# One layer with sampled latent attention: keys turned by VectorE in 32x32 blocks, scores in 32x32 tiles, inversion masks made by GpSimd

## The reference

```
# prompt, gated linear attention in chunks of 64 tokens
lower = where(strict, (kb @ kc^T) * decay, 0)
wy    = solve(eye + lower, eye)                 # unit triangular, 64x64
u, w  = wy @ vb, wy @ (kb * exp(gc))
for each of the 4 chunks: v_new = u - w @ S; o = ...; S = S * exp(g) + k^T v_new

# the 8 sequences, latent attention over 16 cached pages of 128 tokens
q_lat = einsum('bthd,rhd->bthr', q_nope, w_uk)
s     = (q_lat . lat + q_pe . kpe) * MLA_SCALE      # 4 heads, 256 + 64 wide
p     = softmax(s over the cached tokens and the new one)
o     = (p @ lat) @ w_uv

h = x + concat(y_gdn, y_mla) @ w_out
h = h + cross_attention(h, memory);  h = h + mixture_of_experts(h)
```

## Time and profile before

| | us |
|---|---|
| three timed runs | 1494.47, 1496.4, 1496.8 |
| median | 1496.4 |
| span of the profiled execution | 1494.2 |
| PE busy in the span | 1373.9 |
| DVE, ACT, POOL busy | 460.2, 201.1, 42.6 |
| inversion, scan, third stage | 153.6 to 202.0, 203.6 to 270.7, 270.7 to 320.3 |

### The profile page before, as it was taken

The page is one execution under the profiler, slowest core; times in us unless marked ns, Lnnn a source line. Parts: engine busy times, 40 slices in busy tenths (PEclk is TensorE's granted clock), DMA queues, the critical chain, the costliest instruction groups (busy, mean ns, idle before and its releaser), DMA issues.

```text
span 1494.2 us, 21159 instructions
## 1 busy us (share of the span) xinstructions
PE 1373.9 (92%) x8579; PEld 694.5 (46%) x8579; DVE 460.2 (31%) x1116; ACT 201.1 (13%) x399; POOL 42.6 (3%) x37
## 2 busy tenths in 40 slices
PE   8999899899998989999999988989989889899896
PEld 7668766555486453333333333333433333333332
DVE  1856643553024252113113112111221131122213
ACT  1053322321012440000000000000000000000002
POOL 0000101000000320000000000000000000000000
PEclk9999999999999989999999999999999999999999
DMA  9111534448365669999999999999999999999996
GB/s 367 39 53 57 199 143 149 184 150 329 141 253 180 225 276 413 389 413 424 426 425 424 428 425 424 427 424 426 425 424 429 423 424 426 424 426 427 424 426 245
DMA packets 96727, 490.73 MB, mean 328 GB/s; under 512 B 9307, under 2 KB 14527, under 8 KB 61626
## 3 DMA queue, kind: packets, MB, share of 16 engines
q1 hardware_dynamic: 94074, 468.89, 76.8%
q0 software_dynamic: 2304, 20.97, 3.6%
q10 hardware_dynamic: 296, 0.11, 0.0%
HBM read 484.01 MB, written 6.04 MB: 328 GB/s over the span
## 4 chain that ended last, share of the span: by engine, by line
PE 40%; DMA 18%; DVE 6%; issue 2%; SPq 1%; ACT 1%; POOL 1%; DVEq 0%
PE ps L2039 17%; DMA arena<-in_w_e 17%; PE ps L2076 14%; PE ps L2032 2%; PE ps L2064 1%; DVE arena L2604 1%; DVE arena L2614 1%; DVE arena L2611 1%; PE ps L2088 1%; DVE arena L2612 1%; SPq L1467 1%; DMA arena<-in_cache_mem_k 1%; PE ps L2104 1%; PE ps L2118 1%; PE ps L2112 0%
## 5 line engine op out<-in xcount | busy, mean ns | idle before, releaser
L2039 PE MATMUL ps<-arena 128*64 128x512 f32 x2048 | 454.3, 595 | 22.1 <-DMA arena<-in_w_e 21.5
L2039 PEld LDWEIGHTS ps<-arena 128*64 128x64 f32 x2048 | 148.9, 137 | 303.5 <-issue 278.5
L2076 PE MATMUL ps<-arena 128*64 128x512 f32 x952 | 214.2, 604 | 2.4 <-ACT arena L2291 2.4
L2076 PEld LDWEIGHTS ps<-arena 128*64 128x64 f32 x952 | 77.9, 141 | 136.1 <-issue 123.3
L2611 DVE TENSOR_SCALAR arena<-ps 128x1024 f32<-128x1024 f32 x15 | 18.4, 1225 | 243.5 <-PE ps L2039 243.5
L2032 PE MATMUL ps<-arena 96*128 96x512 bf16 x96 | 35.3, 488 | 46.0 <-DVE arena L2604 46.0
L2623 DVE COPY arena<-ps 128x512 f32<-128x512 f32 x15 | 10.4, 692 | 216.5 <-PE ps L2076 216.5
L2629 DVE TENSOR_TENSOR res<-res,ps 128x512 f32<-128x512 f32 x60 | 41.3, 688 | 115.9 <-PE ps L2088 115.9
L2025 PEld LDWEIGHTS ps<-arena 128*128 128x128 bf16 x768 | 49.5, 99 | 14.0 <-issue 12.2
L1753 PE MATMUL ps<-arena 128*128 128x512 f32 x128 | 55.8, 594 | 0.0
L2025 PE MATMUL ps<-arena 128*128 128x128 bf16 x768 | 54.0, 222 | 1.7 <-DVE arena L2578 1.7
(11 more groups left out here) (553 smaller groups left out, 1533.0 us busy)
## 6 DMA issues: line engine op xcount, KB each, us to landing
arena<-in_w_e SPq DMA_DIRECT2D x383, 1024.0 KB, 18.0
arena<-in_w_in SPq DMA_DIRECT2D x8, 1380.0 KB, 17.6
arena<-in_cache_mem_k SPq DMA_DIRECT2D x8, 1024.0 KB, 8.9
arena<-in_w_out SPq DMA_DIRECT2D x2, 2048.0 KB
arena<-in_w_xk SPq DMA_DIRECT2D x1, 4096.0 KB, 15.9
arena<-in_w_xv SPq DMA_DIRECT2D x1, 4096.0 KB, 13.8
arena<-in_w_xq SPq DMA_DIRECT2D x1, 4096.0 KB, 23.2
arena<-in_cache_mem_v SPq DMA_DIRECT2D x1, 4096.0 KB, 16.1
```

The source lines that it names most:

```text
L2039: last = pe.matmul(ps[64 * x:64 * x + 64, c, :], xe[:, k, 64 * x:64 * x + 64], weights[x][:, c * 512:(c + 1) * 512], start=False, stop=(k ...
L2076: last = pe.matmul(ps[64 * x:64 * x + 64, 4 + c, :], aT[:, k, 64 * x:64 * x + 64], weights[x][:, j * D + c * 512:j * D + (c + 1) * 512], s ...
```

## The change

The steps become 24, and what is in them changes. One, the queries of a sequence are scaled once and copied to four groups of 32 rows (`q_spread`, by a product with the constant `C_SAME`). Two, PE no longer turns keys: DVE transposes the gathered tiles in 32x32 blocks, one instruction of 128x1024 for a unit (a fifth of a sequence: 64 of its 320 feature columns, all 16 tiles), one step ahead, into one of four buffers. ACT copies nothing for it. Three, a unit's scores are eight products of K = 32, M = 4 and N = 512 (16 instructions), each on one 32x32 tile of the array; an even sequence uses tiles with equal row and column group, an odd one those two columns further, and 18 of the 24 steps hold a unit of each of two sequences, 4 hold one. A sequence has its own PSUM bank out of three. Four, the maximum is taken per partition by DVE, spread over the row groups by another `C_SAME` product, and reduced again; P is turned by DVE too. Five, the masks of the levels 1 to 5 are packed and made by POOL, behind the gathers of sequences 1 and 2. Six, there is a fourth slot for a sequence; sequence 3 is gathered when the last product of the inversion is done, the later ones after `pv_done` 1 to 4. Seven, the halves of `w_out` are loaded apart: the second at the start of the third stage, the first (the heads of the gated attention) when all values are done, because the fourth slot lies in its place.

```diff
-ARENA = 45680
+ARENA = 45680 + 3072 + 188
+SCRATCH = 4096
...
+    lat_slots.append(Arena(arena, AT_SLOTS + 6 * 1024).take([P, TILES, KVR]))
+    kr_slots.append(Arena(arena, AT_MORE).take([P, TILES, ROPE]))
...
-    def level_part(dve, m, t):
-        for half in HALVES:
-            mask = cst[half, C_LVL + m * P + half.start:C_LVL + m * P + half.stop]
-            last = nc.vector.tensor_tensor(CTc[half, t], LT[half, t, :, half], rep1(mask, [CHUNK, H, CHUNK]), ALU.mult)
-        return last
+    def level_part(eng, m, t):
+        return eng.tensor_tensor(CTc[:, t], LTc[:, t], rep1(c_(C_LVL + m * CHUNK, CHUNK), [P, H, CHUNK]), ALU.mult)
...
+                    pe.wait_ge(ml["q_apart"], 1)
+                    pe.matmul(ps[:, 3, 64:320], c_(C_SAME), q_apart[:, 0:256], start=True, stop=True)
+                    pe.matmul(ps[:, 3, 320:384], c_(C_SAME, P, ROPE), q_apart[0:ROPE, 256:320], start=True, stop=True).then_inc(ml["q_spread"], 1)
...
+    PIECES = 5
+    STEPS = PIECES * DEC // 2 + 4
+    def first_step(b):
+        return PIECES * (b // 2) + 2 * (b % 2)
...
+    def score_bank(b):
+        return 5 + b % 3
+    def pages_pe(pe, k):
+        here = step_units(k)
+        if here:
+            pe.wait_ge(sa["keys"], max(numbered[unit] for unit in here) + 1)
+            for b, m in here:
+                if m == 0 and b >= 3:
+                    pe.wait_ge(sa["exp"], b - 2)
+            for c in range(2):
+                for b, m in here:
+                    d = 2 * m + c
+                    for a in range(4):
+                        rows, out = slice(32 * a, 32 * a + 32), 32 * ((a + 2 * (b % 2)) % 4)
+                        last = pe.matmul(ps[out:out + H, score_bank(b), :], q_spread[rows, d, b, :],
+                                         KT[rows, numbered[b, m] % KEYS, c].rearrange("p s n -> p (s n)"),
+                                         start=(d == 0), stop=(d == 2 * PIECES - 1), tile_position=(32 * a, out))
             last.then_inc(sa["scored"], 1)
...
+            pe.wait_ge(sa["top"], b + 1)
+            if b > 0:
+                pe.wait_ge(sa["acc_moved"], b)
+            at = KVR + 4 * (b % 2)
+            pe.matmul(ps[:, 4, at:at + 4], c_(C_SAME), tops[:, b % 2], start=True, stop=True).then_inc(sa["spread"], 1)
+        for b in values_of(k):
+            pe.wait_ge(sa["p_turned"], b + 1)
...
+    def turn_keys_of(dve, k):
+        for b, m in step_units(k):
+            n = numbered[b, m]
+            if m == 0:
+                dve.wait_ge(seq_loaded[b % NSLOT], 32 * (b // NSLOT + 1))
+            if n >= KEYS:
+                dve.wait_ge(sa["scored"], units[n - KEYS][0] + 1)
+            rows = lat_slots[b % NSLOT][:, :, 64 * m:64 * m + 64] if m < 4 else kr_slots[b % NSLOT]
+            nc.vector.transpose(KT[:, n % KEYS], rows.rearrange("p s (c n) -> p c s n", c=2)).then_inc(sa["keys"], 1)
+    def pages_dve(dve, k):
+        for b in softmax_of(k):
+            dve.wait_ge(sa["scored"], k)
+            dve_chain.link(dve, nc.vector.tensor_reduce(lmax[:, b:b + 1], ps[:, score_bank(b), :], AX, ALU.max))
+            nc.vector.tensor_scalar(tops[:, b % 2], c_(C_GROUP, 4), lmax[:, b:b + 1], None, ALU.mult).then_inc(sa["top"], 1)
+        for b in values_of(k):
+            dve.wait_ge(sa["exp"], b + 1)
+            if b > 0:
+                dve.wait_ge(sa["pv_done"], b)
+            nc.vector.transpose(PT.rearrange("p s n -> p (s n)"), Pb).then_inc(sa["p_turned"], 1)
+        turn_keys_of(dve, k + 1)
+        for b in softmax_of(k):
+            at = KVR + 4 * (b % 2)
+            dve.wait_ge(sa["spread"], b + 1)
+            nc.vector.tensor_reduce(nmax[:, b:b + 1], ps[:, 4, at:at + 4], AX, ALU.max, negate=True).then_inc(sa["max"], 1)
...
-            for b in range(1, NSLOT):
+            for b in (1, 2):
                 load_sequence(pool, b)
-            for k in range(STEP_SCAN):
-                sampled_pool(pool, k)
+            for m in range(1, LEVELS):
+                for t in range(2):
+                    if m > 1:
+                        pool.wait_ge(y_made, 2 * (m - 2) + t + 1)
+                    level_part(nc.gpsimd, m, t).then_inc(c_ready, 1)
+            pool.wait_ge(uw_made, 3)
+            load_sequence(pool, 3)
...
-                    if m > 1:
-                        pe.wait_ge(c_ready, 2 * (m - 2) + t + 1)
+                    pe.wait_ge(c_ready, 2 * (m - 1) + t + 1)
...
-            for half in range(2):
-                load_w_out(sp, half)
+            load_w_out(sp, 1)
             store(sp, gdn_prompt[0, 0].rearrange("h k v -> k h v"), S[:, :, :])
-            sp.wait_ge(sa["pv_done"], DEC)
+            sp.wait_ge(sa["pv_done"], 6)
             sp.dma_start(memt, mem_prompt[0].rearrange("(t p) d -> p t d", p=P)).then_inc(mem_loaded, 16)
             sp.dma_start(wk, w_xk[0].rearrange("(k p) n -> p k n", p=P)).then_inc(wk_loaded, 16)
+            sp.wait_ge(sa["pv_done"], DEC)
+            load_w_out(sp, 0)
...
             pe.wait_ge(gn["placed"], 1)
+            pe.wait_ge(wout_loaded, 32)
             mix_part(0, range(H))
```

More of the change, by code:

```diff
@@ new lines, in build, with step_units @@
+    sa = {n: sem("smla_" + n, True) for n in ("keys", "scored", "top", "spread", "max", "exp", "p_turned", "pv_done", "acc_moved")}
+    PIECES = 5
+    STEPS = PIECES * DEC // 2 + 4
+    def first_step(b):
+        return PIECES * (b // 2) + 2 * (b % 2)
+    def step_units(k):
+        return [(b, k - first_step(b)) for b in range(DEC) if 0 <= k - first_step(b) < PIECES]
+    units = [(k, b, m) for k in range(STEPS) for b, m in step_units(k)]
+    numbered = {(b, m): n for n, (_, b, m) in enumerate(units)}
@@ new lines, in pages_act @@
+    def pages_act(act, k):
+        for b in softmax_of(k):
+            act.wait_ge(sa["max"], b + 1)
+            if b > 0:
+                act.wait_ge(sa["p_turned"], b)
+            for rows, dst in (((slice(0, P), slice(0, P)),), ((slice(64, P), slice(0, 64)), (slice(0, 64), slice(64, P))))[b % 2]:
+                last = nc.scalar.activation(Pb[dst, :], ps[rows, score_bank(b), :], ACT.Exp, bias=nmax[rows, b:b + 1],
+                                            accum_out=lsum[dst, b:b + 1])
+            last.then_inc(sa["exp"], 1)
+        for b in values_of(k):
+            act.wait_ge(sa["pv_done"], b + 1)
+            nc.scalar.copy(acc[:, b, :], ps[:, 4, 0:KVR]).then_inc(sa["acc_moved"], 1)
@@ L1155, in build, with level_step, head_step @@
+    def level_step(m):
+        return m - 1
+    STEP_SCAN = LEVELS
+    PER_CHUNK = 3
+    def chunk_steps(i, second):
+        k = STEP_SCAN + PER_CHUNK * i
+        return range(k + 1, k + PER_CHUNK) if second else range(k, k + 1)
+    STEP_HEAD = STEP_SCAN + PER_CHUNK * (SEQ // CHUNK)
+    def head_step(h):
+        return STEP_HEAD + 2 + h
+    assert head_step(H) == STEPS
     x_turned, x_ready = sem("inv_turned"), sem("inv_x_ready")
@@ L1244, in _ @@
                     last.then_inc(z_made, 1)
[L1245 to L1246 removed]
+            pages_pe(pe, level_step(LEVELS))
             for t in range(2):
@@ L1385, in join_exps @@
         act.wait_ge(jn["max"], 1)
-        nc.scalar.activation(part, part, ACT.Exp, scale=MLA_SCALE)
-        nc.scalar.activation(own, own, ACT.Exp, scale=MLA_SCALE).then_inc(jn["exp"], 1)
+        nc.scalar.activation(part, part, ACT.Exp)
+        nc.scalar.activation(own, own, ACT.Exp).then_inc(jn["exp"], 1)
     def join_weights(dve):
@@ L1549, in _ @@
         def _(pool):
-            for k in range(STEP_HEAD, STEPS):
-                sampled_pool(pool, k)
             pool.wait_ge(cx["q_made"], KD)
```

274 lines of the change are left out of this document (88 added, 186 removed).

## The result

Slower: 1518.28 us median of four runs (1514.24 to 1522.66) against 1495.67 for the kernel before (1494.47 to 1496.8, four runs). The ratio is 1.0152, 95% interval 1.0128 to 1.0176: 22.6 us too many, where 5.9 fewer were forecast, and outside the range.

A forecast was written before the change was run, and what follows sets the result against it. TensorE was taken to bound the three attention stages and DMA of expert weights the end, passing changes on one to one. Terms 0.5 - 5.0 - 4.9 - 5.5 + 6 + 3 = -5.9 gave 1490.5 us by the median, range 1481 to 1513.

The forecast's parts named there:

- before 153 us: Work ahead of the inversion: DVE gains five small operations and three products, loses half-masks; +0.5 us (0 to 1.5).
- inversion, to the end of PE: Inversion stage: first product waits for POOL's mask, then shorter levels; TensorE ends at 197.0 against 201.97, -5.0 us.
- barrier and scan, to the third stage: Scan: DVE sets about 15.0 us a chunk against 16.75, chunk 0 has a new wait; 62.1 against 67.0, -4.9 us.
- third stage, to 311.83: Third stage: six steps with turns and a last score, 15.2 us, become 8.1; -5.5 us (-7 to -2.5).
- to the memory keys: `w_out` and clock: After the last values: new wait for the first half of `w_out`, +6 us; lower clock after three new waits, +3.
- the wait for sequence 3: Scan, chunk 0: the gather lands at 206.8, TensorE waits 3 us and the next turn is late by 1.6.
- The clock: After three new waits (first level, chunk 0, `w_out`) TensorE runs at the lower clock: +3 us (0 to +5).
- the price of a double step: Attention scores: a step with two units, eight tiles side by side, 32 instructions, takes 2.0 us.
- four at once: Rival, score steps: two tiles in one row group take turns, a double step takes 3.8 us; 1513, chance 0.09.
- row tiles in turn: Rival, score steps: a sequence's four tiles write one bank in turn, 155 us in place of 43.6; some 1602, chance 0.04.
- two passes: Rival, DVE turns: a 32-bit transpose needs two passes, 2.45 us a turn; 1512, chance 0.10.
- the waits eat it: Rival: ISA instruction at 4.3, chunk 0 at 7, third stage at -2.5 add 7.8 us; 1498, chance 0.15.

The follow-up runs named there:

- the pad alone: A pad of 32 bytes a partition ahead of the arena, against the kernel before, nothing else changed: 1512.44 us, ratio 1.0115.

## Why the prediction was wrong, step by step

The sum is set against the starts of the stages in the two timelines (the earlier trace rows and above) and of the first memory key, before and after:

```profile
L1753 PE MATMUL ps<-arena x128: 592/592/697, 354.1 to 411.4; 128*128 128x512 f32 x128
```

```profile
L1739 PE MATMUL ps<-arena x128: 592/592/697, 355.7 to 413.0; 128*128 128x512 f32 x128
```

| term | forecast | measured |
|---|---|---|
| before 153 us | +0.5 | +2.4 |
| inversion, to the end of PE | -5.0 | -7.8 |
| barrier and scan, to the third stage | -4.9 | +3.9 |
| third stage, to 311.83 | -5.5 | -6.9 |
| to the memory keys: `w_out` and clock | +9 | +10 |
| experts and the end | 0 | +16.6 |

**The step that failed** is the one ahead of all terms: "what the three stages gain or lose, the end gains or loses one to one, and nothing is won in the last 930 us". It took the pace of the weight stream as given, since no line of that stage changes. But the change re-plans the memory of a partition, and the stream depends on where its destination begins: 425 GB/s on a multiple of 256 bytes, 417 to 418 at 32, 64 or 128 past it. That is 1.1% of the time, shown by the pad alone, and it is three quarters of the result. With the place repaired, one to one holds to about 1 us in the kernels above. The other quarter is the front, where a gain was forecast and 5.8 us were lost; the terms further down are about that.

The Trainium skill ("DMA: Bandwidth & Descriptors", How a descriptor splits into AXI transactions) says that a descriptor which does not start on a 256-byte boundary pays for the bytes from the boundary below it, and speaks there of reads. The unit of 256 agrees with the runs here, in which the source stays and the destination moves; whether the cause is that splitting no run here shows.

**The barrier was mis-sized.** The working kept the 1.64 us of before and put the wait for sequence 3 inside the scan, 3 + 1.6. As the program was written the landing was waited for at the block's end by every engine: 10.50, and the next score step at the lower clock (3.34 in place of 1.92). The scan itself, from 207.10 to 269.21, took 62.1 us against 67.1: the forecast's size, but by luck. The wait for sequence 3 and its 1.6 aren't in it; two costs that the working had not stand there instead, steps at the lower clock (3.41 for 1.92 at 234.27) and 3.01 us at the next barrier. And DVE didn't set the chunk at 15.0: one without such a step takes 13.2 us from one state subtraction to the next, near the 13.4 worked out for TensorE, and DVE waits for PE at both ends.

```profile
240.60 0.68 DVE L1272 TENSOR_TENSOR arena<-arena,ps 64x512 f32<-64x512 f32 x1 [2.53 <-PE ps L1295]
...
253.77 0.69 DVE L1272 TENSOR_TENSOR arena<-arena,ps 64x512 f32<-64x512 f32 x1 [0.79 <-PE ps L1295]
```

With the gather moved, the wait was where the working had it, but of 6.37 (5.89, 6.52 and 4.24 in the three kernels built on that one), for 3, at least in part since the gather, now behind the barrier, was issued 2.3 us after the inversion's end (200.55 against 198.28), where the working had it at that end.

**Before 153 us:** DVE was priced, PE not. The spreading of the queries, L695 and L696 at 146.75, holds PE to 148.52, at a granted clock of 0.50, the level of 1.2 GHz, after 1.18 us without work (the kernel before has that level in this stretch too, 0.50 from 145 to 150).

```profile
146.75 1.22 PE L695 MATMUL ps<-arena,cst 128*128 128x256 f32 x2
```

```profile
146.70:148.60 1.90, 1.90 (x7) 1.08 (x6) 0.00 (x0) 0.11 (x1) 0.00 (x0) 0.50 0.00 0
```

**`w_out`** was right in kind and near in size (7.47 for 6), and the kernel with the mix ahead shows that the order of the mix could hide all of it. **The clock** was right in kind and too small: the eight products behind that wait alone took 6.17 for 3.70, 2.5 of the 3 us put in for all waits. The first level lost 1.5 (a Y of 1.97 for 1.15, a single step of 2.63 for 1.90), the steps at 207.10 and 234.27 1.4 and 1.5, and behind the third stage's barrier L1686 took 5.96 (granted clock 0.51 from 268 to 272) where the same products of before took 3.67:

```profile
271.20 3.67 PE L1702 MATMUL ps<-arena 128*8 128x128 f32 x127
```

These come to 9 us for 3 (range 0 to 5), though the kernel before had such stretches too (206 to 208), so not all of it is the change's. Only the 2.5 lie in the table's row of `w_out`, and the others in the rows ahead.

**Right:** the price of a double step (1.92 for 2.0) and of a single one (1.90 for 1.9), so eight 32x32 tiles run at once, four of them into one bank; with that "four at once" (decided at 2.4) and "row tiles in turn" fall. A turn of keys takes 1.2 (1215 ns mean, two in a row 2.32 to 2.37), so "two passes" falls.

The Trainium skill ("TensorEngine Tiling (Array Packing)", Restrictions and Gotchas) says that row tiles can't use one bank at once. Here four row groups wrote to one bank in different groups of partitions, and at 60 ns an instruction, against 440 for a full array, this trace does not agree.

**The inversion:** the masks were held by the gathers of POOL, as the working had it, and the first Y came at 162.22 for 161.9, though the stage and its gathers began 2.4 us late: between the end of the last gather (161.33) and the first mask (161.43) lie 0.1 us, not the 2 taken for the ISA instruction. (The gap of 4.33 that gave its upper bound ended, by the row's own bracket, with ACT.) The five levels, to the step at 190.53, took 28.3 us for 29.3. One was long, 6.6 at the lower clock, the next three took 5.5, 5.9 and 5.9 for 5.85, and the last 4.5, since it makes only one half of Z (32 products at 189.46, 1.15 us), which the working had priced whole. Because of the late start the table shows 7.8 us won, where by the time of the trace PE ended at 196.6 for 197.0.

**The third stage** won 6.9 for 5.5, inside its range of 2.5 to 7.

**The rivals:** "the waits eat it" came nearest for the front, by another wait than it named: the barrier's.

Open remain the 1.72 us behind "issue", and why the executions of one kernel differ by up to 8 us at the experts' start.

## What to carry to other kernels

When a change frees or packs memory, look where the buffers behind it now begin: a stream that sets the pace for 900 us lost 2% of it to 32 bytes, in a stage that the diff does not touch. At the end of a block, ask what each engine's last instruction waits for: a gather that is issued last makes its landing everybody's wait, and moved behind the barrier it is at least partly covered. Only when placement, barrier and order of the mix were put right did the cheap turns and scores show, at 0.9935 of the time before, and with the first masks at 0.9903.

## What was not expected of the hardware

The stream of 1 MB expert transfers takes 425 GB/s where its tile begins on a multiple of 256 bytes of a partition and 417 to 418 where it begins 32, 64 or 128 bytes past one; a multiple of 512 gives nothing more. Scores on eight 32x32 tiles, 32 instructions of 512 columns, take 1.92 us, 60 ns each. A change of tile shape, from the 64x64 products to such a step and back, shows no gap: the step of 1.92 us starts at 187.60 and the next 64x64 product at 189.46.
